# Sums of squares on VectorE, an earlier evacuation, and a reordered start of the head phase

## What is computed

```python
for l in range(DEPTH):                                   # 2 layers
    h = rms_norm(x, p['norm_mix_pre'][l])
    mix = mixer_ab(h, ...) if l == 0 else mixer_c(h, ...)  # conv + attention | gated recurrence (8 heads)
    x = x + rms_norm(mix, p['norm_mix_post'][l])
    h = rms_norm(x, p['norm_ffn_pre'][l])
    fo, fs = conv_ffn(h, ffn_prev[l], ...)               # (gelu(conv(a)) * b) @ w_down, a, b = h @ w_up
    x = x + rms_norm(fo, p['norm_ffn_post'][l])

def rms_norm(x, g):
    return x * lax.rsqrt(jnp.mean(x * x, axis=-1) + EPS) * g
```

## Time and profile before

| | |
|---|---|
| median of 3 runs | 1330.3 us |
| profiled execution | 1330.19 us, span of the instructions 1328.4 us |
| PE busy | 1313.3 us, 99% |
| DVE busy | 801.2 us, 60% |
| ACT busy | 597.1 us, 45% |
| POOL busy | 186.5 us, 14% |
| granted PE clock | full in all 40 slices |

### The profile page before, as it was taken

The page is one execution under the profiler, slowest core; times in us unless marked ns, Lnnn a source line. Parts: engine busy times, 40 slices in busy tenths (PEclk is TensorE's granted clock), DMA queues, the critical chain, the costliest instruction groups (busy, mean ns, idle before and its releaser), DMA issues.

```text
span 1328.4 us, 31859 instructions
## 1 busy us (share of the span) xinstructions
PE 1313.3 (99%) x12604; PEld 1281.7 (96%) x12604; DVE 801.2 (60%) x1458; ACT 597.1 (45%) x1211; POOL 186.5 (14%) x320
## 2 busy tenths in 40 slices
PE   9999999999999999999999999999999999999998
PEld 9998999999999999997999999989999999999998
DVE  6476576655655632228988888968565566552223
ACT  5367355333333322237766666646433333332232
POOL 0111121111111100000211111111111111120000
PEclk9999999999999999999999999999999999999999
DMA  8312231233222322212333233331133222332211
GB/s 293 115 50 65 81 95 51 93 95 87 86 80 94 116 97 88 81 49 88 115 102 107 97 97 98 110 119 63 51 93 95 85 89 79 101 122 88 87 44 68
DMA packets 39637, 123.23 MB, mean 93 GB/s; under 512 B 4184, under 2 KB 12120, under 8 KB 39448
## 3 DMA queue, kind: packets, MB, share of 16 engines
q1 hardware_dynamic: 34808, 111.37, 26.6%
q10 hardware_dynamic: 4592, 10.56, 2.3%
q0 software_dynamic: 176, 0.44, 0.1%
HBM read 113.78 MB, written 8.57 MB: 92 GB/s over the span
## 4 chain that ended last, share of the span: by engine, by line
PE 89%; DVE 6%; ACT 2%; issue 1%; DMA 0%; POOL 0%; SPq 0%; DVEq 0%; ACTq 0%
PE acc L453 84%; DVE w_lo L1382 1%; PE aux L610 1%; PE aux L764 0%; DVE x L1604 0%; DMA raw<-in_w_in_ab 0%; PE aux L748 0%; ACT w_hi L887 0%; PE aux L792 0%; DVE mix L1599 0%; PE aux L531 0%; PE aux L632 0%; PE aux L622 0%; DVE h_lo L1391 0%; DVE Sst L1785 0%
## 5 line engine op out<-in xcount | busy, mean ns | idle before, releaser
L1382 DVE TENSOR_TENSOR w_lo<-raw,w_hi 128x512 fp32r<-128x512 f32 (+1 forms) x372 | 305.3, 824 | 322.6 <-ACT w_hi L887 322.4
L453 PE MATMUL acc<-h_hi,w_hi 128*128 128x272 f32 x2208 | 474.7, 293 | 3.1 <-DVE h_lo L1391 2.1
L453 PE MATMUL acc<-h_hi,w_lo 128*128 128x272 f32 x2208 | 464.7, 288 | 0.0
L453 PE MATMUL acc<-h_lo,w_hi 128*128 128x272 f32 x2208 | 463.4, 288 | 0.1
L453 PEld LDWEIGHTS acc<-h_hi,w_hi 128*128 128x128 f32 x2208 | 349.8, 188 | 15.2 <-issue 7.4
L887 ACT CAST w_hi<-raw 128x512 fp32r<-128x512 f32 (+1 forms) x372 | 236.3, 642 | 265.2 <-PE acc L453 259.1
L453 PEld LDWEIGHTS acc<-h_lo,w_hi 128*128 128x128 f32 x2208 | 350.0, 189 | 0.2
L453 PEld LDWEIGHTS acc<-h_hi,w_lo 128*128 128x128 f32 x2208 | 348.0, 189 | 0.2 <-issue 0.2
L453 PE MATMUL acc<-g_hi,w_hi 128*128 128x272 f32 x704 | 153.1, 288 | 0.0
L453 PE MATMUL acc<-g_hi,w_lo 128*128 128x272 f32 x704 | 153.0, 289 | 0.0
L453 PE MATMUL acc<-g_lo,w_hi 128*128 128x272 f32 x704 | 152.3, 288 | 0.0
(11 more groups left out here) (266 smaller groups left out, 1346.7 us busy)
## 6 DMA issues: line engine op xcount, KB each, us to landing
raw<-in_w_up SPq DMA_DIRECT2D x88, 512.0 KB, 3.6
raw<-in_w_down SPq DMA_DIRECT2D x32, 704.0 KB, 4.1
raw<-in_w_in_c SPq DMA_DIRECT2D x32, 512.0 KB, 3.6
raw<-in_w_in_ab SPq DMA_DIRECT2D x18, 512.0 KB, 3.9
raw<-in_w_out_ab SPq DMA_DIRECT2D x8, 512.0 KB, 3.6
S<-in_state ACTq DMA_DIRECT2D x8, 512.0 KB, 3.6
o_ss<-Snew ACTq DMA_DIRECT2D x8, 512.0 KB, 2.7
raw<-in_w_out_c SPq DMA_DIRECT2D x8, 512.0 KB, 3.6
```

Of the source, the lines that this page charges most:

```text
L453: mm = pe.matmul(acc[out][:, t, 0:H], w[slot][:, wc], mv[:, kk_, t * H:(t + 1) * H], start=start and k == 0 and q == 0, stop=stop and k == ...
L1382: dve.tensor_tensor(w_lo[slot][:, to], raw[n % 4][:, cols], w_hi[slot][:, to], ALU.subtract).then_inc(lo_ready, 1)
```

## The change

It has four parts.

1. At the two up boundaries PE no longer sums the squares of half 1. DVE adds the eight tiles of squares itself, in three adds of 4, 2 and 1 tiles (squares_added), into S2, right after it has copied half 1 of acc0. PE's statistics product moves from the end of first_pair to the middle of the third unit.
2. At all three boundaries acc0 is evacuated in two pieces: ACT copies half 0 to S0 after tile 2 of half 1 (first_cols), DVE only half 1. The third unit's first two tiles run on half 0, then on half 1.
3. At the in_c boundary PE takes half 0 as tiles 0 to 2 of unit 0, tiles 0 to 2 of unit 1, and then tile by tile for both; the squares of half 1 are summed in two blocks of four; the splits of unit 1 move ahead on ACT and DVE (on DVE from after tiles 4 and 6 to after tiles 2 and 5); ACT computes the root of half 1 ahead of tile 7 of half 0, and copies half 1's sums ahead of half 0's rstd.
4. In the first two pairs of an up phase, ACT and DVE evacuate the third unit (first of pair 1) before tick 3 of pair 0.

```diff
@@ PE, first_pair
-                for e in range(2):
-                    for u in range(2):
...
+                if name == "in_c":
+                    order = [(u, k) for ks in ((0, 1, 2), (3,), (4,), (5,), (6,), (7,)) for u in range(2) for k in ks]
+                else:
+                    order = [(u, 4 * e + k) for e in range(2) for u in range(2) for k in range(4)]
+                for u, k in order:
+                    e = k // 4
+                    if (u, k) == (1, 0):
+                        pe.wait_ge(mix_cols, COLS0[pre + 1])
+                    half(m + 2 * u + e, 0, u, h, 4 * e, e == 0, e == 1, half_ready(pre, 0) if u == 0 else None,
+                         ks=[k % 4], signal=0, ts=(0,), done=first_cols_done if (u, k) == (0, 7) else None)
+                    if (u, k) == ((1, 2) if name == "in_c" else (0, 2)):
+                        stats(norm - 1, 1)
+                square_sums(pre, 0, range(KD))
                 pe.wait_ge(evac, TILE0[name])
                 for k in range(8):
                     e = k // 4
-                    if k == 7:
-                        square_sums(pre, 1)
+                    if name == "in_c" and k == 5:
+                        square_sums(pre, 1, range(4))
+                    if name == "in_c" and k == 7:
+                        square_sums(pre, 1, range(4, KD))
...
-                pre_stats(pre, 1)
+                if name == "in_c":
+                    pre_stats(pre, 1)

             def third_unit(name):

                 m = 2 * (UNIT0[name] + 2)
+                pe.wait_ge(first_cols_copied, RESCALED[name] // 2)
+                for k in range(2):
+                    half(m, 0, 0, h, 0, True, False, ks=[k], signal=0, ts=(0,))
                 pe.wait_ge(evac, TILE0[name] + 1)
-                half(m, 0, 0, h, 0, True, False)
+                for k in range(2):
+                    half(m, 0, 0, h, 0, True, False, ks=[k], signal=0, ts=(1,))
+                half(m, 0, 0, h, 0, True, False, ks=range(2, 4))
@@ PE, ffn
                 third_unit(name)
+                pre_stats(norm // 2, 1)
                 half(2 * (UNIT0[name] + 2) + 1, 0, 0, h, 4, False, True)
@@ ACT
+            def first_cols(pre):
+
+                act.wait_ge(first_cols_done, pre)
+                act.copy(S[0][:, cols(0)], acc[0][:, 0, 0:H]).then_inc(first_cols_copied, 1)
@@ ACT, after_out (up boundaries)
                     normed_square(1, k)
+                    if k == 2:
+                        first_cols(pre)
                     if k == 4:
                         sums_out(pre, 0)
                 norm_root(2 * pre, rstd, 0)
-                sums_out(pre, 1)
                 norm_root(2 * pre, rstd, 1)
@@ ACT, after_down (in_c boundary)
                     normed_tile(pre, 0, k, gain)
-                    if k == 3:
+                    if k == 2:
                         split(m + 2, 0)
                     normed_square(0, k)
...
-                norm_root(post, S[3], 1)
+                    if k == 6:
+                        norm_root(post, S[3], 1)
...
+                sums_out(pre, 1)
                 norm_root(2 * pre, rstd, 0)
-                sums_out(pre, 1)
                 norm_root(2 * pre, rstd, 1)
@@ ACT and DVE, up
+                    ticks = [(u, t) for u in range(2) for t in range(4)]
+                    if first:
+                        ticks = [(0, 1), (0, 2), (1, 0), (1, 1), (0, 3), (1, 2), (1, 3)]
@@ DVE
                     dve.wait_ge(half_done, m + 2 * u + 2)
+                    if u == 0 and name != "in_ab":
+                        dve.tensor_copy(out[:, cols(1)], acc[0][:, 1, 0:H]).then_inc(evac, 1)
+                        if name != "in_c":
+                            squares_added(RESCALED[name] // 2)
+                        continue
...
+            def squares_added(pre):
+
+                q = cols(1)
+                dve.wait_ge(sq_pre, x_count(pre, 1, KD - 1))
+                step.mark(dve.tensor_tensor(sq_c[:, 0:4, q], sq_c[:, 0:4, q], sq_c[:, 4:8, q], ALU.add))
+                step.wait(dve)
+                step.mark(dve.tensor_tensor(sq_c[:, 0:2, q], sq_c[:, 0:2, q], sq_c[:, 2:4, q], ALU.add))
+                step.wait(dve)
+                dve.wait_ge(sums_taken, {1: 1, 3: 5}[pre])
+                dve.tensor_tensor(S[2][:, q], sq_c[:, 0, q], sq_c[:, 1, q], ALU.add).then_inc(sums_taken, 1)
@@ DVE, after_down (in_c boundary)
-                        if t == 0 and k in (0, 1, 4, 6):
-                            split(m + {0: 0, 1: 1, 4: 2, 6: 3}[k], 0)
+                        if t == 0 and k in (0, 1, 2, 5):
+                            split(m + {0: 0, 1: 1, 2: 2, 5: 3}[k], 0)
```

More of the change, by code:

```diff
@@ L515, in first_pair, with square_sums @@
                         pre_stats(pre, 0)
-                pre_stats(pre, 1)
+                if name == "in_c":
+                    pre_stats(pre, 1)
             def third_unit(name):
                 m = 2 * (UNIT0[name] + 2)
+                pe.wait_ge(first_cols_copied, RESCALED[name] // 2)
+                for k in range(2):
+                    half(m, 0, 0, h, 0, True, False, ks=[k], signal=0, ts=(0,))
                 pe.wait_ge(evac, TILE0[name] + 1)
-                half(m, 0, 0, h, 0, True, False)
-            def square_sums(pre, t):
+                for k in range(2):
+                    half(m, 0, 0, h, 0, True, False, ks=[k], signal=0, ts=(1,))
+                half(m, 0, 0, h, 0, True, False, ks=range(2, 4))
+            def square_sums(pre, t, ks):
                 sq = sq_c
-                pe.wait_ge(rstd_ready, 4 * pre - 2 + t + 1)
-                for k in range(KD):
+                if 0 in ks:
+                    pe.wait_ge(rstd_ready, 4 * pre - 2 + t + 1)
+                for k in ks:
                     j = k % 4
@@ L532, in square_sums @@
                                    start=k < 4, stop=k >= 4)
-                mm.then_inc(sq_summed, 1)
+                if KD - 1 in ks:
+                    mm.then_inc(sq_summed, 1)
             def pre_stats(pre, t):
@@ L925, in norm_root @@
                 src = A[2 + t if pre else t][:, 0:H]
+                by_tiles = pre and (t == 0 or norm == 4)
                 act.wait_ge(stat_done, 2 * norm + t + 1)
-                step.mark(act.activation(out[:, cols(t)], src, ACT.Ln, bias=eps[:], scale=1.0 / (32 * D if pre else D)))
+                step.mark(act.activation(out[:, cols(t)], src, ACT.Ln, bias=eps[:],
+                                         scale=1.0 / (32 * D if by_tiles else D)))
                 step.wait(act)
@@ L1176, in up @@
                 def up(i, s_off, first=False):
-                    for u in range(2):
-                        pair = CA + KF * layer + u + 2 * i
-                        for t in range(4):
+                    ticks = [(u, t) for u in range(2) for t in range(4)]
+                    if first:
+                        ticks = [(0, 1), (0, 2), (1, 0), (1, 1), (0, 3), (1, 2), (1, 3)]
+                    if True:
+                        for u, t in ticks:
+                            pair = CA + KF * layer + u + 2 * i
                             for q in halves_at(t, first and u == 0, True):
@@ L1733, in up @@
                                                   ).then_inc(g_ready, 1)
-                base = step.n
                 up(0, 0, True)
-                per = step.n - base
-                base = step.n
+                base, per = step.n, 4
                 with dve.Fori(1, KF // 2 - 1) as i:
```

5 lines of the change are left out of this document (4 added, 1 removed).

## The result

The changed kernel takes 1331.91 us (median of 20 runs, 1331.53 to 1333.63), the kernel before 1330.11: ratio 1.0015 (1.0014 from the two medians), 95% interval 1.001 to 1.0021. One execution of the kernel before (5648.7 us) and one of E5 (4799.1 us) were far slower than all others and stand outside the ratios. The forecast was 1331.4. The profiled execution has a span of 1331.1 (before 1328.4), the granted clock is 1.0 in both.

The account below looks back on a forecast made before the run. PE's instructions and waits were taken to bound the kernel, with VectorE setting the pace at in_c. Ups -0.1 and in_c +1.3 gave +1.2 us on 1330.19, forecast 1331.4 us; range 1327.9 to 1333.2.

Parts of the forecast that it names:

- Step 1: Up boundaries, PE: 1.25 us of square sums and 0.32 us of evacuation wait go, 1.57 us gained at each.
- Step 2: Up boundaries, VectorE: three adds take 1.32, 0.73 and 0.43 us; sum ready at 214.63, moved product at 214.84 without waiting.
- rival 3: Up boundaries: VectorE's adds take far more than 2.5 us; at 4.0 each loses 1.3, giving 1334.0 us; chance 0.10.
- Step 3: After up boundaries: unit 3's evacuation is late, PE waits 1.5 us at unit 5; net gain 0.06 us each.
- Step 4: in_c: VectorE idles 1.19 us for ACT's cast before the third split; head 0 +1.39, loss taken as +1.3 us.
- The bound of +0.2 without the cast: in_c: low bound of the loss, +0.2 us, if ACT's cast is not in VectorE's way.
- Rival 1: First pairs have slack: both up boundaries keep 1.57 us, in_c still loses 1.3; 1328.5 us; chance 0.19.
- Rival 2: Change does what it says: ups gain 3.1 us, in_c gains 0.7; 1326.5 us; chance 0.15.

Follow-up runs that it names:

- E5: Changed kernel with the first pairs' order on VectorE and ACT as in the kernel before, both up phases: 1335.71 us, ratio 1.0041.
- E8: Changed kernel with in_c as in the kernel before and unit 2 evacuated straight after the first convolution at the ups: 1327.32 us, ratio 0.9979.
- E12: Kernel before plus only the half-by-half evacuation of acc0 and third unit's start on half 0, at both ups: 1329.92 us, ratio 0.9999.
- E3: Changed kernel with one more, unused add of 128x4x272 in VectorE's first-pair chain of both up phases: 1334.28 us, ratio 1.0029.
- E4: Changed kernel with unit 2 evacuated straight after the first convolution, weight splits moved behind it, both up phases: 1329.41 us, ratio 0.9992.
- E7: Changed kernel with ACT's cast for in_c's third split one tile earlier: 1330.92 us, ratio 1.0008.
- E6: Changed kernel with the second half's square sums back on PE in both up phases: 1329.1 us, ratio 0.9991.
- E11: E6 with one more, long-satisfied semaphore wait at the start of PE's program: 1329.53 us, ratio 0.9995.
- E9: Kernel before with three more, long-satisfied semaphore waits in PE's program: 1330.29 us, ratio 1.0003.
- E10: E8 with three more, long-satisfied semaphore waits in PE's program: 1328.0 us, ratio 0.9982.
- E1: Changed kernel with its in_c part undone, both up boundaries as changed: 1330.52 us, ratio 1.0004.
- E2: Kernel before with only the changed in_c boundary, both ups as before: 1331.72 us, ratio 1.001.

## Why the prediction was right

**Step 1, PE's account, 1.57 us at each up boundary: right.** Unit 4's last matmuls are issued at 229.98 and 0.25 behind would be 230.23; the step said PE arrives at 230.33. Units 3 and 4 start 1.54 earlier than in before, and in E8, where nothing holds PE, units 5 and 6 too. The part of 0.32 for the evacuation is right as well: E12 has it alone, 0.32 at unit 3, and loses 0.23 of it by unit 6, since the evacuation of unit 3, 0.34 ahead of unit 5 in before, then comes too late.

**Step 2, VectorE's adds: right.** 1.32, 0.76 and 0.36 from start to start, against 1.32, 0.73 and 0.43; the sum is there at 214.5 and the moved product runs at 214.74 without a wait (foretold 214.84). E3 is rival 3 made real: the adds take 3.8 us in all, PE waits 1.0 there, and each boundary loses 1.2 to 1.3, which rival 3 gave for 4.0.

**Step 3, the chain to unit 5: right in each link.** Foretold and measured: scaling of S0 216.55, 216.44; gelu 220.09, 219.98; gate product 220.83, 220.71; evacuation of unit 2 223.26, 223.15; of unit 3 231.07, 230.91; unit 5 231.84, 231.76; PE's wait 1.5, 1.36. All are early by 0.1 to 0.2, and so is the trace ahead of them. That VectorE's split stands still beside POOL's product decides this step. Two splits take 2.05 us in after and 1.29 in before, and in E4, where the splits keep clear of the first product, one takes 0.70 and a pair 1.29. The Trainium skill, "SBUF — State Buffer", section "SBUF: two separate sides", says that whichever of the two starts first keeps the shared ports for its whole instruction; these rows agree.

The prediction says of the split of 229.48 that it ends with POOL's product; its row ends at 230.92, 0.55 behind the product's end of 230.37, and the sum rightly has it so. What the step lacked is the 0.09 that PE loses behind the wait, until the second pair of matmuls: the gain of 0.06 at each boundary became a loss of 0.09.

**Step 4, in_c: right in place, the loss a little larger.** Idle 1.10 for 1.19, third split 599.46 for 599.49, second half 608.69 for 608.75, head 0 at +1.44 for the +1.39 of the chain; I took +1.3. The bound of +0.2 without the cast was low: E7 leaves 0.72, and less the 0.34 for which VectorE still waits it would be 0.4, an estimate. The cast is held from both sides, by ACT's order and by the place for the weights (597.90), which no row of mine looked at; and PE's own part between the two statistics products, the squares in two blocks, came to 0.33 where I had 0.21. No run has the squares in one block with all else kept.

**Rivals.** Rival 1 (slack) fell with E3, where 1.33 us more cost 1.2 to 1.3. Rival 2 (it does what it says) fell at the waits of 1.4 us; E8 shows that its ups were to be had with another order. The sum, +1.2, stands against +1.5 in the spans and +1.8 in the medians: 0.15 is in_c, 0.2 that the ups brought +0.1 and not -0.1, and 0.3 lies outside the span and has no cause here. The stop of 1.00 us in the last head, which four of the 20 executions seem to have, was in no step either; that the median leaves it out is luck.

## What to carry to other kernels

When work is moved off a busy engine, follow the engine that takes it until its next hand-over back: here PE saved 1.5 us at a boundary and waited 1.4 us 20 us later for a tile whose evacuation had become late by the same adds. Then look at the order behind those adds before giving up the idea: the evacuation of unit 2 stood behind two splits that could wait, and moving it ahead of them took 2.5 us off (E4); with in_c left alone besides, the loss of 1.8 us became a gain of 3.0 (E8). And an instruction that two engines must both do in turn (cast, then split) is as early as the later of the two queues and as the place that it writes to.

## What the hardware showed beside that

A pair of 128x272 matmuls took 0.2500 us in the up and down phases of two kernels (E6, E11) and 0.2505 to 0.2506 in those of all the others, at the same granted clock; it is 1.07 us in each of the two long phases, as much as most edits here are worth. Neither three more instructions in PE's program nor the same matmuls at the boundary carried it over (E9, E10, E12). This is open.

The stop of 1.00 us in the last head stands in the profiles of after, E4 and E5 and in none of the other eleven, though E1, E3, E7 and E8 run the same matmuls there. The DMA queue that the profile calls instruction tells them apart. It brings blocks of 16 KB; `--dma --window 868:870` of after has one of them and nothing else:

```profile
q8 instruction: 1, 0.02, 3.0%
```

Its start against the matmul behind the stop (the fifth of the 64), from the traces:

| kernel | block starts | behind the one before | fifth matmul | distance |
|---|---|---|---|---|
| after | 869.07 | 7.17 | 871.42, after a stop | 2.35 |
| E4 | 867.36 | 7.01 | 869.71, after a stop | 2.34 |
| E5 | 870.77 | 7.50 | 873.12, after a stop | 2.35 |
| E3 | 867.99 | 5.21 | 871.55 | 3.57 |
| E1 | 863.60 | 3.79 | 868.69 | 5.09 |
| E7 | 864.24 | 3.77 | 869.37 | 5.13 |
| E8 | 862.26 | 3.77 | 867.38 | 5.12 |

In all three PE goes on 2.35 us behind the start of a late block, within 0.01, and where the block starts 3.57 us or more ahead there is no stop; in the seven kernels not listed the distance is 4.71 to 5.16. Five kernels (before, E2, E6, E9, E11) have shorter stops of this kind in the head phase, 0.12 to 0.39 us, and they end 2.3 to 2.6 us behind such a start. So PE very likely stands there for its own next instructions. No run moved a block on purpose, and why it is late in some executions stays open.
